# Gated convolution layer on one core: first weights in common pieces, and another order of GpSimd's and VectorE's steps ahead of the output product

## The reference, cut to what matters

```python
hn = rms_norm(x, norm_g)
z = hn @ w_in                       # 1024 x 3072
a, b, gate = jnp.split(z, 3, axis=-1)
u = a * jax.nn.sigmoid(b)
u = conv(u, conv_w) + conv_b        # causal, 31 taps, each channel by itself
mu, var = mean(u), mean((u - mu) ** 2)           # over the channels of a token
uf = (u - mu) * lax.rsqrt(var + LN_EPS) * ln_g + ln_b
v = jax.nn.silu(uf) * jax.nn.silu(gate)
out = x + v @ w_out
```

## Time and profile before

| | |
|---|---|
| median of 3 runs | 356.37 us (356.23 to 356.69) |
| profiled execution | 356.49 us |
| its span, first to last instruction | 354.7 us |
| outside the span | 1.8 us |
| granted TensorE clock | 1.0 of full speed |

### The profile page before, as it was taken

One profiled execution on the slowest core, in us unless ns is written; L12 is line 12 of the kernel. 1 busy time (PEld: TensorE's weight loads), 2 busy tenths in 40 slices (PEclk: granted clock), 3 DMA queues, 4 the chain that ended last, 5 costly groups with the idle time before them and its releaser, 6 DMA issues.

```text
span 354.7 us, 4758 instructions
## 1 busy us (share of the span) xinstructions
PE 349.1 (98%) x1564; PEld 288.6 (81%) x1564; DVE 323.1 (91%) x514; ACT 232.2 (65%) x334; POOL 270.2 (76%) x194
## 2 busy tenths in 40 slices
PE   8999999999999999999999999999999999999996
PEld 7878888888888888888888888888788877888886
DVE  4779799999999999989999998997699999999972
ACT  6899684667936870998659777976774872443400
POOL 0129999999999998789999999885698551359240
DMA  7995011211410321404120411341733497046152
GB/s 255 404 412 225 33 61 59 71 50 59 118 61 10 91 80 59 118 2 118 59 60 6 115 59 31 99 109 61 234 121 119 138 416 276 2 136 219 63 206 90
DMA packets 30520, 43.51 MB, mean 123 GB/s; under 512 B 18336, under 2 KB 18848, under 8 KB 30496
## 3 DMA queue, kind: packets, MB, share of 16 engines
q1 hardware_dynamic: 30352, 43.21, 36.7%
q10 hardware_dynamic: 144, 0.00, 0.0%
HBM read 34.82 MB, written 4.19 MB: 110 GB/s over the span
## 4 chain that ended last, share of the span: by engine, by line
PE 82%; DVE 8%; issue 3%; DMA 2%; SPq 2%; ACT 2%; DVEq 0%; ACTq 0%
PE mm L634 63%; PE acc L713 9%; PE mm L713 8%; DMA sgate<-x 2%; DVE nat L1207 2%; DVE x_lo L1243 2%; PE mm L651 2%; SPq L496 1%; DVE sgate L1236 1%; DVE nat L1228 1%; ACT mm L939 1%; DVE sgate L1263 1%; DVE nat L1275 0%; SPq L522 0%; ACT sgate L775 0%
## 5 line engine op out<-in xcount | busy, mean ns | idle before, releaser
L634 PE MATMUL mm<-x_hi,w_hi 128*128 128x512 f32 x352 | 137.4, 390 | 0.0
L634 PE MATMUL mm<-x_hi,w_lo 128*128 128x512 f32 x352 | 137.0, 389 | 0.0
L634 PE MATMUL mm<-x_lo,w_hi 128*128 128x512 f32 x352 | 136.9, 389 | 0.0
L1187 DVE SCALAR_TENSOR_TENSOR acc<-u,chan,acc 128x512 f32<-128x512 f32 x157 | 110.4, 747 | 0.1
L1496 POOL TENSOR_TENSOR pconv<-pconv,prod 128x512 f32<-128x512 f32 x60 | 78.2, 1344 | 1.3 <-ACT prod L870 1.3
L634 PEld LDWEIGHTS mm<-x_hi,w_hi 128*128 128x128 f32 x352 | 66.1, 188 | 13.6
L634 PEld LDWEIGHTS mm<-x_hi,w_lo 128*128 128x128 f32 x352 | 66.1, 188 | 13.7
L634 PEld LDWEIGHTS mm<-x_lo,w_hi 128*128 128x128 f32 x352 | 66.1, 188 | 13.6
L1187 DVE SCALAR_TENSOR_TENSOR acc<-u,w_sum,acc 128x512 f32<-128x512 f32 x90 | 67.2, 746 | 2.4 <-ACT acc L852 2.3
L870 ACT ACTIVATE prod<-u,chan 128x512 f32<-128x512 f32 x69 | 48.0, 716 | 19.9 <-POOL pconv L1496 18.4
L1440 POOL TENSOR_TENSOR w_lo<-raw,w_hi 128x1024 fp32r<-128x1024 f32 (+1 forms) x21 | 50.2, 2390 | 8.8 <-ACT w_hi L819 8.8
(11 more groups left out here) (109 smaller groups left out, 536.2 us busy)
## 6 DMA issues: line engine op xcount, KB each, us to landing
raw<-w_in SPq DMA_DIRECT2D x22, 512.0 KB, 3.4
nat<-x_t SPq DMA_DIRECT2D x16, 256.0 KB, 6.2
sgate<-x SPq DMA_DIRECT2D x8, 512.0 KB, 10.2
raw<-w_out SPq DMA_DIRECT2D x8, 512.0 KB, 3.3
nat<-x SPq DMA_DIRECT2D x8, 512.0 KB, 6.8
y<-nat SPq DMA_DIRECT2D x15, 256.0 KB, 2.2
raw_late<-w_out SPq DMA_DIRECT2D x4, 512.0 KB, 3.8
sig<-w_out SPq DMA_DIRECT2D x4, 512.0 KB, 4.3
```

Source lines behind the costliest of these rows:

```text
L634: ins = nc.tensor.matmul(bank(("unit", m, h)), w[:, m % 3, k, :], xx[:, k, half(h)], start=(k == 0 and i == 0), stop=(k == KC - 1 and i == 2))
L1187: ins = nc.vector.scalar_tensor_tensor(dst, chain_in(j, chain, k), tap(j, chain, k), chain_bank(j, chain), ALU.mult, ALU.add)
```

## The change

Five things are changed:

1. The first two units' weights come from an input of their own, `w_first`, in four pieces of 256 KB as before; a piece now holds two slices `k` of both units. The loads and splits stand ahead of slices 0, 2, 4 and 6 (before: 0, 1, 4 and 5). PE takes, for each slice, x hi by weight hi of both units, then x hi by weight lo of both, then x lo by weight hi of both.
2. DVE makes two diagonals ahead of slice 4 and two ahead of slice 5 (before three and one).
3. POOL computes each half's inverse deviation ahead of the "lo" operation instead of after it, does its six `scale`s in a row, and "lo" (1, 0) and (1, 1) after them.
4. The pause for DVE's first four lo parts of v moves from "22-12" (2, 0) to "lo" (1, 0).
5. `post` (1, 0) stands ahead of the four `sum_v` (2, k) (before: after the first), `post` (1, 1) ahead of the four `split_v` (2, k) (before: after the second).

```diff
-DIAGS_BEFORE = {4: (4, 5, 6), 5: (7,)}
+DIAGS_BEFORE = {4: (4, 5), 5: (6, 7)}
...
-W_PAUSES = {("22-12", 2, 0): CK, ("lo", 2, 0): 2 * CK, ("21-", 3, 0): 4 * CK, ("12-11", 5, 0): 5 * CK, ("lo", 6, 0): 7 * CK}
+W_PAUSES = {("lo", 1, 0): CK, ("lo", 2, 0): 2 * CK, ("21-", 3, 0): 4 * CK, ("12-11", 5, 0): 5 * CK, ("lo", 6, 0): 7 * CK}
...
-FIRST_PIECES = ((0, 0), (1, 0), (0, 1), (1, 1))
-PIECES_BEFORE = {0: (0,), 1: (1,), 4: (2,), 5: (3,)}
...
+FIRST_PIECES = 4
+PIECE_BEFORE = {0: 0, 2: 1, 4: 2, 6: 3}
...
-                m, part = FIRST_PIECES[i]
-                kind, j = UNITS[m]
-                cols = first_columns(part)
-                sp.dma_start(raw[:, m, cols], w_in[PART[kind], j, :, cols]).then_inc(w_first_in[i], 16)
+                sp.dma_start(first_raw(i), w_first[i]).then_inc(w_first_in[i], 16)
...
-                    sp.wait_ge(w_first_lo, 3)
+                    sp.wait_ge(w_first_lo, FIRST_PIECES // 2)
...
-                if h == 1:
-                    for m, k, i in FIRST_TERMS:
-                        raw_term(m, 1, k, i)
-                for k in range(2 if h == 1 else 0, KC):
-                    for m in range(2):
-                        for i in range(3):
+                for k in range(KC):
+                    for i in (0, 2, 1):
+                        for m in range(2):
                             ins = raw_term(m, h, k, i)
...
+            posts(1, (0,))
             for k in range(CK):
                 sum_v(2, k)
-                if k == 0:
-                    posts(1, (0,))
+            posts(1, (1,))
             for k in range(CK):
                 split_v(2, k)
-                if k == 1:
-                    posts(1, (1,))
...
-            w_out_op(*W_OPS[0])
             for h in range(NH):
                 inverse_deviation(h)
-            w_out_op(*W_OPS[1])
-            for k in POOL_SCALES[0]:
-                scale(k, 0)
-            w_out_op(*W_OPS[2])
-            w_out_op(*W_OPS[3])
-            for k in POOL_SCALES[1]:
-                scale(k, 1)
-            for op in W_OPS[4:]:
+                w_out_op(*W_OPS[h])
+            for h in range(NH):
+                for k in POOL_SCALES[h]:
+                    scale(k, h)
+            for op in W_OPS[2:]:
```

More of the change, by code:

```diff
@@ L95, with gated_conv_layer @@
                for b, part, q in POSTS}
-FIRST_PIECES = ((0, 0), (1, 0), (0, 1), (1, 1))
-PIECES_BEFORE = {0: (0,), 1: (1,), 4: (2,), 5: (3,)}
-FIRST_TERMS = ((0, 0, 0), (0, 0, 2), (1, 0, 0), (0, 0, 1), (1, 0, 1), (1, 0, 2), (0, 1, 0), (1, 1, 0),
-               (0, 1, 2), (1, 1, 2), (0, 1, 1), (1, 1, 1))
+FIRST_PIECES = 4
+PIECE_BEFORE = {0: 0, 2: 1, 4: 2, 6: 3}
 WARM_UPS = 11
-def gated_conv_layer(nc, x, x_t, w_in, w_out, per_channel, identity, out):
+def gated_conv_layer(nc, x, x_t, w_first, w_in, w_out, per_channel, identity, out):
     T, D = x.shape
@@ L213, in gated_conv_layer @@
         norm_in = sem("norm_in")
-        w_first_in = [sem(f"w_first_in{i}") for i in range(4)]
+        w_first_in = [sem(f"w_first_in{i}") for i in range(FIRST_PIECES)]
         w_first_hi = sem("w_first_hi")
@@ L409, in rms_spread, with first_raw, first_raw_units, first_units @@
             return acc[:, 3 - h, :]
[L411 to L417, removed]
+        def first_raw(i):
+            return raw[:].rearrange("p m c -> p (m c)")[:, HALF * i:HALF * (i + 1)]
+        def first_raw_units(i):
+            return first_raw(i).rearrange("p (m c) -> p m c", m=2)
+        def first_units(w, i):
+            ks = KC // FIRST_PIECES
+            return w[:, 0:2, ks * i:ks * (i + 1), :].rearrange("p m k n -> p m (k n)")
         def nth(kind, m):
@@ L517, in load_first_weights @@
             def load_first_weights(i):
-                m, part = FIRST_PIECES[i]
-                kind, j = UNITS[m]
-                cols = first_columns(part)
-                sp.dma_start(raw[:, m, cols], w_in[PART[kind], j, :, cols]).then_inc(w_first_in[i], 16)
+                sp.dma_start(first_raw(i), w_first[i]).then_inc(w_first_in[i], 16)
             for k in range(KC):
-                for i in PIECES_BEFORE.get(k, ()):
-                    load_first_weights(i)
+                if k in PIECE_BEFORE:
+                    load_first_weights(PIECE_BEFORE[k])
                 load_columns(1, k)
@@ L639, in raw_term @@
             def raw_term(m, h, k, i):
-                piece = FIRST_PIECES.index((m, k // (KC // 2))) + 1
+                piece = k // (KC // FIRST_PIECES) + 1
                 if i == 0:
@@ L651, in raw_term @@
                 return nc.tensor.matmul(bank(("unit", m, h)), w[:, m, k, :], xx[:, k, half(h)],
-                                        start=(k == 0 and i == 0), stop=(k == KC - 1 and i == 2))
+                                        start=(k == 0 and i == 0), stop=(k == KC - 1 and i == 1))
             def project_raw(h):
-                if h == 1:
-                    for m, k, i in FIRST_TERMS:
-                        raw_term(m, 1, k, i)
-                for k in range(2 if h == 1 else 0, KC):
-                    for m in range(2):
-                        for i in range(3):
+                for k in range(KC):
+                    for i in (0, 2, 1):
+                        for m in range(2):
                             ins = raw_term(m, h, k, i)
-                        if k == KC - 1:
-                            ins.then_inc(unit_ready[UNITS[m][0]], 1)
+                            if (k, i) == (KC - 1, 1):
+                                ins.then_inc(unit_ready[UNITS[m][0]], 1)
                     if (h, k) == SPREAD_AT[1]:
@@ L784, in split_first @@
             def split_first(i):
-                m, part = FIRST_PIECES[i]
                 act.wait_ge(w_first_in[i], 16)
-                nc.scalar.activation(w_hi[:, m, first_ks(part), :].rearrange("p k n -> p (k n)"),
-                                     raw[:, m, first_columns(part)], ACT.Copy).then_inc(w_first_hi, 1)
+                nc.scalar.activation(first_units(w_hi, i), first_raw_units(i), ACT.Copy).then_inc(w_first_hi, 1)
             def rms_diagonal(t):
@@ L959, in _ @@
             for k in range(KC):
-                if k > 0:
-                    for i in PIECES_BEFORE.get(k, ()):
-                        split_first(i)
+                if k > 0 and k in PIECE_BEFORE:
+                    split_first(PIECE_BEFORE[k])
                 split_raw(1, k)
```

10 lines of the change are left out of this document (4 added, 6 removed).

## The result

The changed kernel takes 359.29 us, median of 4 runs (358.67 to 359.86), against 356.47 for the kernel before: ratio 1.0079 with a 95% interval of 1.0060 to 1.0098, so 2.8 us (2.1 to 3.5) slower. The forecast was 358.6, slower. The profiled execution is the longest of the four: 359.86 us for a span of 358.1, against 356.49 and 354.7 before. In the experiments one execution of the kernel before (1254.87 us) and one of e11 (1254.72 us) were slow and are left out of the ratios.

A forecast was written before the change was run, and what follows sets the result against it. PE and DVE both nearly full until 255 us, DVE's list to 294, then PE. Span 354.7 + 2.9 - 0.65 = 356.95, plus 1.8 outside gives 358.7, median 358.6 us; range 357.1 to 359.8.

The forecast's parts named there:

- steps 3 and 4: POOL's new order and pause: DVE's first splits gain 2.1 us, but reloads and ACT's list make the gates 2.15 us later.
- The lock: DVE's two-input splits stand still until POOL's instruction ends, through an exclusive shared port; block 1's splits last until 286.6.
- At a quarter of its speed: Alternative reading of DVE's splits beside POOL, slowing in proportion; the sum would come out about 1 us higher.
- a margin of 0.4 us: At block 1's splits: POOL begins at 279.6, 0.4 before DVE at 280.0, so POOL goes first.
- x's rows: x's first rows, queued behind "22-12" (2, 1), land at 292.2 and hold `post` (1, 0): +1.1 us.
- The rival by which these rows are no wait: x's first rows do not hold `post` (1, 0); +1.85 - 0.65, 357.5 us; 14% chance.
- The start and the diagonals: Steps 1 and 2: L624 at 24.0 at best, and -0.65 us carried to the convolution's end (bounds 0 and -0.85).
- the wait at slice 4: PE's wait at 23.26 for x lo of slice 4 goes with two diagonals ahead instead of three: 0.5 us.
- PE's part: PE starts block 2 at 298.8 instead of 297.0, 1.8 late, and becomes late by 2.9 at 330.41.
- DVE's delay: DVE and POOL 2.95 us late at block 2 (2.15 + 1.1 - 0.3); 2.9 of it reaches the end through PE.
- again short of 333: Expected profile sign: PE idles a us or more ahead of piece (1, 2), and again shortly before 333.
- the rival in which the lock falls the other way: DVE's split comes first at 280.0, and "22-12" (2, 1) ends 0.6 to 0.9 later: 359.4 us; 12% chance.

The follow-up runs named there:

- e11: Kernel before with only DVE's diagonals made two ahead of slice 4 and two ahead of slice 5: 356.42 us, ratio 0.9997.
- e3: Changed kernel with only the pause put back ahead of "22-12" (2, 0), GpSimd's new order kept: 355.98 us, ratio 0.9979 to the kernel before.
- e9: Changed kernel with the pause one place later, between "lo" (1, 0) and "lo" (1, 1): 356.54 us, ratio 1.0009 to the kernel before.
- e1: Kernel before with only GpSimd's part of the change, its new order and the moved pause: 359.47 us, ratio 1.0086.
- e7: Changed kernel with x's first two rows asked for ahead of block 3's loads: 357.77 us, ratio 1.0040 to the kernel before.
- e8: Changed kernel with ten unused matmuls added in PE's idle ahead of piece (1, 2): 359.15 us, ratio 1.0072 to the kernel before.
- e5: Kernel before with only the new pieces of the first two units' weights and PE's new order of terms: 356.03 us, ratio 0.9986.
- e4: Changed kernel with the pause behind both "lo" of block 1 and ahead of half 1's scales: 355.49 us, ratio 0.9973 to the kernel before.

## Why the prediction was right, point by point

**The main step, steps 3 and 4, held link by link.** The changed kernel's convolution ends 0.37 earlier than before (DVE's centring at 255.14, has 255.51), so 0.37 is added to its rows here to compare with the forecast's clock. In brackets is the forecast: "22-12" (2, 0) ends 281.9 (282.0), "22-12" (2, 1) 284.7 (284.8), `act_norm` 2 begins 285.7 (285.8), the last gate ends 291.1 (291.1). The splits of block 0 took 2.49 (2.48). That the pause is the cause is shown by e3 (pause back, loss gone) and e9 (one instruction less behind it, 2.5 us less). That it works through ACT's list is read from the timelines: both `split_w_out` wait for GpSimd, 2.21 and 1.75 us, and in e1, where x's row holds DVE for only 0.28, the first sum still comes 2.1 us later than before. No run moved ACT's two splits by themselves.

**The lock.** The forecast took DVE's two-input split to stand still during GpSimd's instruction, and to lose nothing beyond it. The split at 279.60 lasted 2.50, GpSimd's at 279.16 only 2.39, no longer than without company. At a quarter of its speed beside GpSimd, DVE would have done most of the split by 281.55 and ended it near 281.7, not at 282.10 (an estimate from these rows). That is the exclusive lock of the Trainium skill, "SBUF — State Buffer", section "Who interferes with whom", and not a slowing in proportion; the trace agrees. Which of the two goes first was forecast rightly at a margin of 0.4 us, and it fell so in the changed kernel, where GpSimd was 0.44 ahead; e1, e7 and e8 have the same long group of splits (6.4 to 6.5 us).

**x's rows, mis-sized.** The term was +1.1 us, as 7.4 us from the end of "22-12" (2, 1) to the landing. It was 8.1 (284.36 to 292.46). The first row took 6.75 us from issue to landing where the earlier trace rows has 6.0. The loads ahead of it are the same, and e1 has 6.0 for it and e8 7.0, so this is scatter between executions; what makes it was not settled. The idle of DVE is 1.79. That is 0.7 us more loss than forecast. The rival by which these rows are no wait is wrong, and e7 shows their share, 1.5 us.

**The start and the diagonals, -0.65.** In the changed kernel's own profile this was -0.37, at `scale_gate` and at the end of the convolution alike, so it was passed on whole, as forecast. Over nine profiles with the new start the mean is -0.53 at `scale_gate` and -0.38 at the centring, and e5 measures -0.5 at the end. The failed part is its split. I gave 0.5 of the 0.65 to the diagonals and the wait at slice 4; e11 has 0.3 for them at L624 and nothing that can be measured at the end, and the new pieces and order of terms bring what there is. The size at the end was a little too large, and one profile would have told this wrongly, as my expectation of e5 shows.

**PE's part.** The forecast had PE 1.8 late at block 2 and catching up to DVE's delay by 330. In the trace block 2 begins at 300.50 instead of 297.09: PE is 3.4 late at once (3.8 in the forecast's clock), since its clock fell behind the idle, which the forecast did not name. So PE never had to catch up, and was not "again short of 333": it takes the second lo part at 333.82, DVE having ended it at 333.58. The way to the end was another, the end the same, since DVE's delay of 3.3 us (splits of block 3) is as long; e8 shows both. That the missing term left the sum alone is luck: with DVE less late, as in e1, it costs some 0.6 us.

**The sum.** 2.9 for DVE's delay was 3.3 + 0.37 = 3.7 in the profile (splits of block 2 done at 298.66 instead of 295.36), 0.65 was 0.37, together +3.3 instead of +2.25 in the slowest of four executions; the median is +2.8. The two errors have the same sign. The 359.29 lies in the stated range, but just above the 358.0 to 359.2 that the forecast gave for its own mechanism, near the 359.4 of the rival in which the lock falls the other way. That rival did not occur: GpSimd went first. What is over comes from x's rows and from the start.

## What to carry to other kernels

A pause that spares one engine's work is priced by all that stands in a row behind it: here two instructions, a reload of 3.3 us and two more, and then two other engines' lists that stand in order. With the other parts of the change in place, the pause was put in four places: ahead of "22-12" (e3) -0.7 us, ahead of half 1's scales (e4) -1.0, between both "lo" (e9) +0.3, ahead of both "lo" +2.8. Put it where the work behind it has slack rather than where a buffer is waiting to be reloaded; which of the two good places is better is not shown. In an in-order load queue, look for loads whose place is already free standing behind ones that must wait; moving two of them gave 1.0 to 1.5 us.

## What of the hardware was not expected

**The granted clock after a short idle.** In the changed kernel PE idled 3.30 us, ran 1.2 us at full clock, and then had 0.54 of it for 3.7 us, as the windows above show; from 294.9 to 297.9 alone it is 0.50, the lower level of 1.2 GHz. e1, with an idle of 2.53 us, shows the lower level too. Windows of e1:
```profile
293.90:295.00 1.10, 1.10 (x4) 0.90 (x3) 1.10 (x3) 1.10 (x3) 0.00 (x0) 0.50 1.03 421
295.00:296.00 1.00, 1.00 (x4) 0.74 (x3) 1.00 (x3) 1.00 (x3) 0.00 (x0) 0.50 1.07 438
```
The kernels with idles of 1.39 (e7), 1.21 (e9) and 0.89 (e8) at this place kept 1.00. What exactly decides it was not tried.

**The first loads scatter.** With the same code ahead of it, ACT's hi part of slice 1 began at 5.50 in one profile and at 6.85 in another. Over the nine profiles with the new start `scale_gate` began between 36.45 and 37.51, and not in the order in which that slice landed; what moves it stays open. A term of half a microsecond at the start of a kernel can't be read from one profile.
